# Seven early units of the up-projection instead of six, and two key loads ahead of the conv states and constants

## What is computed

```python
z = x @ w_in                                   # q | k | v | B | C | h
att = attend(q, k, v)                          # prompt: causal; sample: top 3 of 8 key blocks, paged cache
conv_y, _ = causal_dwconv(gc * h, conv_buf, w_conv)
mix = concat([att, gb * conv_y]) @ w_out
x1 = layer_norm(ALPHA * x + mix, ln1_g, ln1_b)
up, _ = causal_dwconv(x1 @ w_up, ffn_buf, w_fconv)   # w_up: 1024 x 5632
a, g = split(up)
y = layer_norm(ALPHA * x1 + (silu(a) * g) @ w_down, ln2_g, ln2_b)
```

## Time and profile before

| | us |
|---|---|
| median of 3 runs | 447.43 (447.05 to 448.56) |
| the profiled execution | 448.32 |
| its span, first to last instruction | 446.5 |
| PE busy | 416.1 (93%) |
| DVE busy | 296.0 (66%) |
| ACT busy | 181.6 (41%) |
| POOL busy | 104.4 (23%) |
| moved by DMA | 124.85 MB, mean 280 GB/s |

### The profile page before, as it was taken

How to read it: one execution, slowest core, us unless ns; L and a number is a source line. 1 busy time by engine, 2 the same in 40 slices (tenths; PEclk the granted TensorE clock), 3 DMA queues, 4 the chain that set the end, 5 groups by cost and what they waited for, 6 DMA issues and landing times.

```text
span 446.5 us, 8259 instructions
## 1 busy us (share of the span) xinstructions
PE 416.1 (93%) x2911; PEld 341.0 (76%) x2911; DVE 296.0 (66%) x383; ACT 181.6 (41%) x694; POOL 104.4 (23%) x133
## 2 busy tenths in 40 slices
PE   4999999999999998999798989999999999999990
PEld 4588887876866774664364369999999999999990
DVE  0496999999799976944351264766666877534536
ACT  1476568653377334011110043455554456224201
POOL 1003033995255231100000436211222221000002
PEclk9999999999999999999999999999999999999997
DMA  8999999999999999999999953566666685968002
GB/s 294 385 329 386 385 388 379 370 357 390 398 386 372 351 393 387 386 386 386 386 377 386 304 166 111 159 178 189 189 182 170 166 215 155 234 174 212 24 1 97
DMA packets 109515, 124.85 MB, mean 280 GB/s; under 512 B 5775, under 2 KB 66920, under 8 KB 109466
## 3 DMA queue, kind: packets, MB, share of 16 engines
q1 hardware_dynamic: 101138, 107.55, 72.5%
q10 hardware_dynamic: 8336, 16.78, 10.5%
HBM read 121.90 MB, written 2.61 MB: 279 GB/s over the span
## 4 chain that ended last, share of the span: by engine, by line
PE 55%; DVE 18%; SPq 11%; issue 6%; DMA 5%; POOL 2%; ACT 1%; DVEq 0%; POOLq 0%; ACTq 0%
PE ps L1815 11%; PE ps L1816 11%; PE ps L1817 11%; SPq L354 8%; DVE qk L930 5%; DVE T L940 5%; PE ps L1432 4%; PE ps L1627 4%; PE ps L1708 3%; PE ps L1603 3%; PE ps L1629 3%; PE ps L1372 3%; DMA wring<-in_cache_v 2%; DMA KV<-in_cache_k 2%; POOL x1l L605 1%
## 5 line engine op out<-in xcount | busy, mean ns | idle before, releaser
L1177 DVE TENSOR_TENSOR wlo<-KV,whi 128x2048 fp32r<-128x2048 f32 (+1 forms) x24 | 61.8, 2576 | 57.1 <-ACT whi L832 29.1
L1432 PE MATMUL ps<-xT,wring 128*128 128x264 f32 x384 | 89.6, 389 | 0.0
L1432 PEld LDWEIGHTS ps<-xT,wring 128*128 128x128 f32 x384 | 71.9, 191 | 13.4 <-issue 1.7
L1815 PE MATMUL ps<-x1h,whi 128*128 128x264 f32 x256 | 73.8, 288 | 0.2
L930 DVE TENSOR_TENSOR qk<-KV,qk 128x1536 f32<-128x1536 f32 (+1 forms) x32 | 67.8, 2122 | 9.2 <-DMA KV<-in_cache_k 5.5
L1817 PE MATMUL ps<-x1h,wlo 128*128 128x264 f32 x256 | 72.7, 284 | 0.0
L1816 PE MATMUL ps<-x1l,whi 128*128 128x264 f32 x256 | 72.7, 284 | 0.0
L662 ACT ACTIVATE qk<-qk 128x64 f32<-128x64 f32 x216 | 51.8, 244 | 28.5 <-POOL qk L553 21.1
L940 DVE TENSOR_REDUCE T<-qk 128x24 f32<-128x1536 f32 (+1 forms) x32 | 58.4, 1827 | 0.0
L1815 PE MATMUL ps<-fh,whi 128*128 128x264 f32 x176 | 50.4, 286 | 0.1
L1816 PE MATMUL ps<-fl,whi 128*128 128x264 f32 x176 | 50.0, 284 | 0.0
(11 more groups left out here) (218 smaller groups left out, 578.9 us busy)
## 6 DMA issues: line engine op xcount, KB each, us to landing
KV<-in_cache_k SPq DMA_DIRECT2D x128, 256.0 KB, 7.3
KV<-in_w_ffn_up SPq DMA_DIRECT2D x32, 512.0 KB, 5.1
KV<-in_cache_v SPq DMA_DIRECT2D x60, 256.0 KB, 8.5
wring<-in_cache_v SPq DMA_DIRECT2D x56, 256.0 KB, 7.5
KV<-in_w_ffn_down SPq DMA_DIRECT2D x8, 1408.0 KB, 7.0
wring<-in_w_in ACTq DMA_DIRECT2D x5, 2048.0 KB, 15.1
zbuf<-in_cache_v SPq DMA_DIRECT2D x12, 256.0 KB, 6.0
zbuf<-in_w_ffn_up SPq DMA_DIRECT2D x3, 1024.0 KB, 11.5
```

Source lines behind the costliest of these rows:

```text
L1177: nc.vector.tensor_tensor(wlo[s][:, 0:n], w2[s][:, 0:n], whi[s][:, 0:n], ALU.subtract).then_inc(s_lo, 1)
L1432: ins = nc.tensor.matmul(ps[:, z_bank(n), 0:R], tile[k], xT[:, k, :], start=k == 0, stop=k == KT - 1)
L1815: nc.tensor.matmul(out, wh[k], xh[k], start=k == 0, stop=False)
```

## The change

There are seven early units and 15 late ones. The additional early unit is number 4, and its weights ("solo") go to the second half of the query buffer by two DMAs with pieces of 512 bytes, issued behind value 20. Units 5 and 6 take the two pairs. TensorE computes both halves of unit 4, the first half of unit 5 and the first half of unit 6 before value 31 (before: the first halves of units 4 and 5). Two of the four `keep_clock` matmuls go. The samples' up-projection of the early units has a fourth group with one unit. The PSUM banks of the down-projection are swapped, as 15 is odd. In the key stage SP issues the first two key slots of sample 1 before the conv states, and the constants in two halves behind the first two key slots of sample 2.

```diff
-E = 6
+E = 7
 QUAD = 4
-ES = E // 2
+ES = (E + 1) // 2
...
+        solo = qk[:, 0, UNIT:2 * UNIT].rearrange("p (k a n) -> p k a n", k=KT, a=2)
...
-            return pairs[a][:, k, (u - QUAD) * P:(u - QUAD + 1) * P]
+            if u == QUAD:
+                return solo[:, k, a, :]
+            return pairs[a][:, k, (u - QUAD - 1) * P:(u - QUAD) * P]
...
-            return 7 if m == 0 else m % 2
+            return 7 if m == 0 else 2 * late_slot(NL) + m % 2
...
-            sp.dma_start(stack[up_tiles, 0:STATE_ROWS, :],
-                         state_ffn_conv[0].rearrange("b k (n d) -> n (b k) d", d=P)).then_inc(s_stack, 16)
...
-            sp.dma_start(stack[mixer_tiles, STATE_ROWS:STACK, :],
-                         w_conv[0].rearrange("k (n d) -> n k d", d=P)).then_inc(s_stack, 16)
...
+            def load_solo():
+                sp.wait_ge(s_kused, NS * SLOTS)
+                sp.wait_ge(s_kpool, pool_pages(NS * SLOTS))
+                for a in range(2):
+                    sp.dma_start(solo[:, :, a, :], wup[:, :, QUAD * P + a * FF:QUAD * P + a * FF + P]).then_inc(s_eu[6], 16)
...
-            load_consts(0, 8)
-            for s in range(SLOTS):
-                load_keys(1, s, ids)
+            load_keys(1, 0, ids)
+            load_keys(1, 1, ids)
+            sp.dma_start(stack[up_tiles, 0:STATE_ROWS, :],
+                         state_ffn_conv[0].rearrange("b k (n d) -> n (b k) d", d=P)).then_inc(s_stack, 16)
...
+            sp.dma_start(stack[mixer_tiles, STATE_ROWS:STACK, :],
+                         w_conv[0].rearrange("k (n d) -> n k d", d=P)).then_inc(s_stack, 16)
+            load_keys(1, 2, ids)
+            load_keys(1, 3, ids)
             for b in range(2, 5):
                 ids = page_ids(b)
                 for s in range(SLOTS):
                     load_keys(b, s, ids)
+                    if b == 2 and s < 2:
+                        load_consts(4 * s, 4 * s + 4)
...
                     if v in (12, 13):
                         load_quad(v - 10)
+                    elif v == 20:
+                        load_solo()
...
-            for u in range(QUAD):
+            for u in range(QUAD + 1):
                 early_scaled(u)
                 silu(u)
...
             for i in range(ES):
                 act.wait_ge(s_es, i + 1)
-                nc.scalar.activation(ev[:, i, :], ps[:, (7, 4, 5, 6)[i], 0:P], ACT.Copy).then_inc(s_ec, 1)
+                n = P if 2 * i + 1 < E else P // 2
+                nc.scalar.activation(ev[0:n, i, :], ps[0:n, (7, 4, 5, 6)[i], 0:P], ACT.Copy).then_inc(s_ec, 1)
...
             sample_columns(5)
+            early_convolved(4)
             masked_values(6)
+            gated(4)
...
-            value_range(21, 23)
+            value_range(21, 22)
+            early_half(3, 1)
+            value_range(22, 23)
             sample_outputs(3)
-            early_half(3, 1)
-            value_range(23, 25)
+            early_half(4, 0)
+            value_range(23, 24)
+            early_half(4, 1)
+            value_range(24, 25)
             sample_outputs(4)
-            early_half(4, 0)
-            value_range(25, 27)
+            value_range(25, 26)
+            early_half(5, 0)
+            value_range(26, 27)
             sample_outputs(5)
-            early_half(5, 0)
-            value_range(27, 30)
+            early_part(6, 0, 0, 4)
+            value_range(27, 28)
+            early_part(6, 0, 4, KT)
+            value_range(28, 30)
             sample_outputs(6)
+            value_range(30, 31)
             pe.wait_ge(s_cv, 2 * QUAD)
             pe.wait_ge(s_tl, QUAD)
-            keep_clock(3, 448)
-            value_range(30, 31)
             keep_clock(3, 512)
-            keep_clock(3, 384)
             value_range(31, 32)
             keep_clock(3, 320)
             sample_outputs(7)
-            early_part(4, 1, 0, 4)
+            early_part(5, 1, 0, 4)
...
-            early_part(4, 1, 4, KT)
+            early_part(5, 1, 4, KT)
...
-            early_half(5, 1)
+            early_half(6, 1)
```

More of the change, by code:

```diff
@@ L415, in load_quad @@
                 sp.dma_start(quads[i], wup[:, k:k + 4, a * FF:a * FF + QUAD * P]).then_inc(s_eu[i], 16)
+            def load_solo():
[3 more added lines that the diff above has]
+                    sp.dma_start(solo[:, :, a, :], wup[:, :, QUAD * P + a * FF:QUAD * P + a * FF + P]).then_inc(s_eu[6], 16)
             def load_pair(a):
                 sp.wait_ge(s_mix, KT)
-                first = a * FF + QUAD * P
+                first = a * FF + (QUAD + 1) * P
                 sp.dma_start(pairs[a], wup[:, :, first:first + 2 * P]).then_inc(s_eu[4 + a], 16)
-            load_consts(0, 8)
-            for s in range(SLOTS):
-                load_keys(1, s, ids)
+            load_keys(1, 0, ids)
+            load_keys(1, 1, ids)
+            sp.dma_start(stack[up_tiles, 0:STATE_ROWS, :],
+                         state_ffn_conv[0].rearrange("b k (n d) -> n (b k) d", d=P)).then_inc(s_stack, 16)
+            sp.dma_start(stack[up_tiles, STATE_ROWS:STACK, :],
+                         w_ffn_conv[0].rearrange("k (n d) -> n k d", d=P)).then_inc(s_stack, 16)
+            sp.dma_start(stack[mixer_tiles, 0:STATE_ROWS, :],
+                         state_conv[0].rearrange("b k (n d) -> n (b k) d", d=P)).then_inc(s_stack, 16)
+            sp.dma_start(stack[mixer_tiles, STATE_ROWS:STACK, :],
+                         w_conv[0].rearrange("k (n d) -> n k d", d=P)).then_inc(s_stack, 16)
+            load_keys(1, 2, ids)
+            load_keys(1, 3, ids)
             for b in range(2, 5):
@@ L816, in early_scaled @@
                 bank = ps[:, u % 4, :].rearrange("p (a n) -> p a n", a=2)
-                act.wait_ge(s_u, QUAD + 1 + u if u < QUAD else 2 * QUAD + 3 + u - QUAD)
+                act.wait_ge(s_u, QUAD + 1 + u if u < QUAD else 2 * QUAD + 2 if u == QUAD else 2 * QUAD + 4 + u - QUAD)
                 if u >= 2:
@@ L847, in _ @@
             normalise(first_rows, 2, s_shift, 2, s_srx)
-            early_scaled(4)
             early_scaled(5)
-            silu(4)
+            early_scaled(6)
             silu(5)
+            silu(6)
             act.wait_ge(s_sr, 1)
@@ L1238, in _ @@
             nc.vector.tensor_tensor(x1l[:, :, NPR:R], new, x1h[:, :, NPR:R], ALU.subtract).then_inc(s_xsh, 1)
-            early_convolved(4)
             early_convolved(5)
-            gated(4)
+            early_convolved(6)
             gated(5)
+            gated(6)
             low(1, UNIT)
@@ L1696, in early_part @@
                     if u == QUAD:
+                        pe.wait_ge(s_eu[6], 32)
+                    elif u == QUAD + 1:
                         pe.wait_ge(s_eu[4 + a], 16)
@@ L1788, in _ @@
             for i in range(ES):
-                units = range(2 * i, 2 * i + 2)
+                units = range(2 * i, min(2 * i + 2, E))
                 for k in range(KT):
@@ L1798, in _ @@
                 pe.wait_ge(s_ec, i + 1)
-                turn(ps[:, 7, i * P:(i + 1) * P], ev[:, i, :]).then_inc(s_et, 1)
+                n = P if 2 * i + 1 < E else P // 2
+                turn(ps[:, 7, i * P:i * P + n], ev[0:n, i, :], n).then_inc(s_et, 1)
             def split_product(out, wh, wl, xh, xl, prompt=None, between=None):
```

7 lines of the change are left out of this document (2 added, 5 removed).

## The result

The changed kernel is slower. Its median is 452.2 us against 447.7 us of the kernel before on the same chip, a ratio of 1.0092 with a 95% interval of 1.0072 to 1.0112. A second series gave 1.0096 (1.0067 to 1.0124). The prediction was 446.9 us with a range that ended at 449.2. So a change forecast at -0.5 us cost 4 to 4.5 us. The profiled execution took 451.4 us with a span of 449.6 us, 3.1 more than the 446.5 of before.

A forecast was written before the change was run, and what follows sets the result against it. DMA stream bounds up to some 252 us, PE's instruction count after 272 us. Terms -5.8 + 3.3 + 0.2 + 1.8 + 0 = -0.5 us take 447.43 to 446.9 us; 8-in-10 range 444.6 to 449.2.

The forecast's parts named there:

- Bound and rule: Before 252 us added bytes cost DMA time, PE work only what overfills its waits; late matmuls are worth 120.5 ns each.
- part 5: Key stage, keys loaded first: gain from closed dips against new PE waits, put at 0 us (bounds -2.1 and +1.7).
- part 4: Joint between value stream and late stage: a fourth sample group adds 1.8 us, all other steps 0.
- Part 1: Late stage: one unit less saves 48 matmuls of 120.5 ns, 5.8 us.
- Part 2: Value stage: the solo load of 1 MiB in 512-byte pieces delays the stream 3.3 us (bounds 2.7 and 3.4).
- Part 3: Value 20 to the last pair: two more halves on PE nearly fit its waits, overhang +0.2 us (bounds 0 and 1.5).
- swallow: Up to 103.36 us: PE's waits of 1.06, 0.41 and 0.86 us for other engines absorb 2.3 us of its new waiting.
- VectorE's lead: Key stage: sample 1's first slot comes some 3 us earlier; VectorE's head start can only close dips, at most 2.1 us.
- The waits at 70.1, 97.6 and 103.4 us: PE's waits for other engines in the key stage, forecast to shrink to nearly nothing.
- the dips: Stretches where SP had nothing to issue, DMA share 0.71 at 88 us and 0.85 at 150 us; forecast to stay.
- rival 1: Key stage: VectorE's lead closes the dips and PE's new waits are shorter, 2.1 us better, 444.8 us; chance 0.21.
- Rival 2: Key stage: constants land after 57.0 us, PE waits 7 us at `lnr`, +4.7, 449.6 us; chance 0.16.

The follow-up runs named there:

- reorder run: Kernel before with six early units, only SP's key-stage load order changed (two key slots ahead of conv states, constants split behind sample 2's first slots): ratio 1.0031.
- unit run: Kernel before with the seventh early unit and all that belongs to it, loads in the old order: ratio 1.0032.
- fillers: Changed kernel plus matmuls that nobody reads, in PE's waits for the states, for the constants and before value 21: ratio 1.0052 against the kernel before.

## Why the prediction was wrong

**Bound and rule: right.** Bytes before the last pair cost stream time, late matmuls bring their full price. The forecast span was -0.5 us and the first profile has +3.1. The 3.6 us between them are, by the marks of the result: the fourth group 1.85, the new order 0.75, the solo load 0.7, PE's overhang 0.6, and the late unit -0.3. The medians add 1.4 us more. So no single step carries the error; the two that failed in kind, not only in size, are part 5 and what part 4 left out.

**Part 1, the late unit: right.** Forecast -5.8, measured -6.1 between the first late matmul and the end.

**Part 2, the solo load: the mechanism right, the term too small.** Forecast 3.3 with an upper bound of 3.4, measured 4.0. The price was read from late loads that ran alone, and SP's part of it was put at "two issues", covered by a backlog. The two issues took 5.27 us and the stream had a window at 362 GB/s behind them. PE's wait before value 21, forecast 1.3, was 2.0 for the same reason.

**Part 3, PE's overhang: the mechanism right, the term too small.** The list runs without a wait from value 21 to the pair, as forecast, and the pair had landed when PE came to it. From value 20 to the pair it is 40.6 us instead of 35.8, so +4.8; less the 4.0 of the load, that leaves 0.8 where 0.2 was put, within its bounds of 0 and 1.5. The list itself takes 33.9 us from value 21 to the pair, where the working has 33.3. The other 1.5 us of 258.2 against the forecast's 255.9 are value 20's 0.75 and the load's 0.7.

**Part 4, the fourth group: the largest miss in the profile.** Forecast 1.8, measured 3.65, of which 1.73 is the gap. I had costed a group at the pitch of the last of three, took for granted that the fourth keeps that pitch, and so put a gap of PE at nothing. The half-filled group does cost like a full one, as I took it: 34 records took 2.01 us.

**Part 5, the new order: failed.** It was put at 0 with -2.1 to +1.7, and alone it cost 1.4 us in the median, inside its bounds. The working had PE's new waits (0 to 1 us and 3.0; measured 1.9 and 2.6), but then let other waits "swallow" 2.3 us of them and set the rest against an imagined gain from VectorE's lead. The waits at 70.1, 97.6 and 103.4 us did vanish, as forecast. The stream was late nonetheless: 1.65 us of 3.0 in the reorder run, and 1.7 in the changed kernel's first profile (value 20 at 217.56) against the unit run's (215.86). The step that failed is the sentence that the stream is never empty at the dips. The working named the later `w_in` loads behind PE's wait and then gave them no price: they are issued 3.2 us later in the changed kernel (91.59 against 88.42), and the dip at 88 us, which was to stay, became a hole down to a share of 0.18. Two of the three waits that were to swallow PE's delay, at 97.6 and 103.4 us, lie behind that issue. The dip at 150 us closed, as rival 1 had it (0.85 to 1.05 in the changed kernel), which gave back only a part. What VectorE's lead brings with the waits taken away can't be told from nothing (0.9989 and 0.9993, both intervals holding 1).

**What wasn't in the sum at all: the clock.** I had read in the earlier trace rows that the granted clock stayed up from 212 to 214 us, where PE did a third of its work, and took from that one row that idling is free. Here it fell to the half level behind waits of 1.8 to 4.0 us in six profiles, but not in the changed kernel's first, and not in the fillers'. The fillers brought 2.0 us of the 4.3 back in the median; that this is the clock and nothing else is argued from the granted clock of the profiles, and the figure is rough.

Rival 2 of the prediction named one of the places, the constants. They landed at 57.31 us, just past the 57.0 that it set as its mark, but PE's wait for them was 2.56 us and not 7, as PE itself came later by its wait for the states; and that wait, put at 0 to 1 us, was the longer one in the reorder run. Its 449.6 us is nearer to the result than the forecast, and by another sum.

## What to carry to other kernels

A load that is moved back is paid at the first instruction in the fixed order of the engine that awaits it, and then by every load that waits for that engine's later work. Before moving it, look which independent work can be put ahead of the wait: where one load group was moved, that alone was worth some 3.6 us with the loads unchanged; where both were, it brought 0.2 in the median, so measure it. A row of short instructions that is made longer can get a gap that the shorter one didn't have, so fold it into fewer and fuller ones before adding to it. And a price taken from a load running alone was too low when the load was put into a full queue: look at what the issuing engine spends on it as well.

## What the runs showed of the hardware that I had not expected

- The same 1 MiB costs the value stream 1.5 us more in pieces of 512 bytes than in rows of 2 KB (value 21 came 6.7 and 5.2 us behind value 20), and its two issues hold SP's queue for 5.27 us instead of 1.69.
- PE's profile has a gap of 0.8 to 1.8 us with no releaser but issue, 4.1 to 6.1 us into a run of records 28 ns apart. Folded into fewer matmuls, the run had none in its 6.2 us; nor had the three groups of the kernel before, 5.4 us long.
- The granted clock went to 0.50 behind waits of 1.8 to 4.0 us in the profiles of six runs, and stayed at 1.00 behind waits of 1.89, 2.56 and 1.99 us in the changed kernel's first profile. The length of the wait alone doesn't decide it, and no run here shows what does.
